# Feed-forwards whose input is turned unnormed, with the reciprocal roots multiplied in behind the first product

## The reference

```python
def rmsnorm(x, g):
    xf = x.astype(jnp.float32)
    y = xf * lax.rsqrt(jnp.mean(xf * xf, axis=-1, keepdims=True) + NORM_EPS)
    return (y * g.astype(jnp.float32)).astype(x.dtype)

def conv_ffn(x, w_in, conv_w, conv_b, w_out):
    T = x.shape[1]
    gate, up = jnp.split(x @ w_in, 2, axis=-1)
    gp = jnp.pad(gate, ((0, 0), (CONV_W - 1, 0), (0, 0)))
    gc = conv_b
    for j in range(CONV_W):
        gc = gc + gp[:, j:j + T, :] * conv_w[j]
    h = jax.nn.gelu(gc) * up
    return h @ w_out
...
        x = x + rmsnorm(m, norm_g[layer, 1])
        f = conv_ffn(rmsnorm(x, norm_g[layer, 2]), ffn_w_in[layer], ffn_conv_w[layer],
                     ffn_conv_b[layer], ffn_w_out[layer])
        x = x + rmsnorm(f, norm_g[layer, 3])
```

## Time and profile before

| | us |
|---|---|
| median of 3 runs | 1328.93 |
| lowest, highest | 1328.87, 1329.26 |
| the profiled execution | 1331.13 |
| its span in the profile | 1329.2 |
| PE busy in it | 1300.9 (98%) |
| DVE busy | 948.4 (71%) |
| ACT busy | 668.1 (50%) |
| from the start of the first product with the diagonal to the first `second`, `ffn0` | 224.19 to 240.46 |
| the same, `ffn1` | 523.57 to 539.83 |

### The profile page before, as it was taken

The page is one execution under the profiler, slowest core; times in us unless marked ns, Lnnn a source line. Parts: engine busy times, 40 slices in busy tenths (PEclk is TensorE's granted clock), DMA queues, the critical chain, the costliest instruction groups (busy, mean ns, idle before and its releaser), DMA issues.

```text
span 1329.2 us, 23254 instructions
## 1 busy us (share of the span) xinstructions
PE 1300.9 (98%) x9190; PEld 1127.4 (85%) x9190; DVE 948.4 (71%) x1646; ACT 668.1 (50%) x1026; POOL 103.2 (8%) x106
## 2 busy tenths in 40 slices
PE   7999999999999999999999998999999999999999
PEld 7889988888888888888888886888888888888887
DVE  6995476877778765877776697866666796666664
ACT  4554326444446586444446476543344568543331
POOL 0005250010000020000001020000001042000000
PEclk9999999999999999999999999999999999999999
DMA  9531107655533423655542631956350431674610
GB/s 301 175 127 65 52 19 253 209 187 189 191 125 135 136 91 127 205 187 189 191 156 82 217 134 44 361 214 236 144 179 11 167 127 64 242 265 154 226 64 32
DMA packets 113350, 208.48 MB, mean 157 GB/s; under 512 B 3952, under 2 KB 57584, under 8 KB 112752
## 3 DMA queue, kind: packets, MB, share of 16 engines
q1 hardware_dynamic: 113264, 207.28, 45.2%
HBM read 206.21 MB, written 1.05 MB: 156 GB/s over the span
## 4 chain that ended last, share of the span: by engine, by line
PE 87%; DVE 6%; ACT 5%; DMA 1%; issue 1%; POOL 0%; SPq 0%; DVEq 0%; ACTq 0%; POOLq 0%
PE ps L1071 21%; PE ps L1018 19%; PE ps L923 10%; PE ps L1023 10%; PE ps L1113 2%; PE ps L1234 2%; PE ps L1499 2%; PE ps L1128 2%; PE ps L1408 1%; DVE Al L2774 1%; PE ps L994 1%; ACT Ah L1947 1%; PE ps L1543 1%; PE ps L847 1%; PE ps L1557 1%
## 5 line engine op out<-in xcount | busy, mean ns | idle before, releaser
L1018 PE MATMUL ps<-hTx,Ah 128*128 128x512 f32 x1088 | 270.7, 391 | 0.0
L2781 DVE TENSOR_TENSOR Al<-ringA,Ah 128x2048 fp32r<-128x2048 f32 x74 | 169.3, 2287 | 97.2 <-ACT Ah L1957 97.2
L1018 PEld LDWEIGHTS ps<-hTx,Ah 128*128 128x128 f32 x1088 | 199.7, 188 | 38.5
L1023 PEld LDWEIGHTS ps<-hTx,Al 128*128 128x128 f32 x1152 | 156.7, 190 | 10.6
L1992 ACT COPY xn<-ps 128x512 f32<-128x512 f32 x72 | 42.3, 587 | 243.4 <-PE ps L1023 236.2
L1023 PE MATMUL ps<-hTx,Al 128*128 128x256 f32 x1152 | 160.7, 282 | 0.0
L1957 ACT CAST Ah<-ringA 128x2048 fp32r<-128x2048 f32 x76 | 145.8, 1918 | 13.1 <-PE ps L923 6.5
L1966 ACT CAST Bh<-ringB 128x1024 fp32r<-128x1024 f32 (+1 forms) x76 | 107.1, 1409 | 89.4 <-PE ps L1071 89.2
L923 PE MATMUL ps<-Ah,hTx 128*128 128x512 f32 (+1 forms) x576 | 136.5, 387 | 2.9 <-ACT Ah L1947 1.4
L2788 DVE TENSOR_TENSOR Bl<-ringB,Bh 128x1024 fp32r<-128x1024 f32 (+1 forms) x76 | 127.0, 1671 | 10.8 <-ACT Bh L1966 10.3
L1071 PE MATMUL ps<-Bh,hidh 128*128 128x512 f32 x416 | 129.9, 392 | 1.1 <-issue 1.1
(11 more groups left out here) (464 smaller groups left out, 2059.5 us busy)
## 6 DMA issues: line engine op xcount, KB each, us to landing
ringA<-in_ffn_w_in SPq DMA_DIRECT2D x44, 1024.0 KB, 6.8
ringA<-in_mlp_w SPq DMA_DIRECT2D x32, 1024.0 KB, 7.4
ringB<-in_mlp_w SPq DMA_DIRECT2D x32, 1024.0 KB, 6.9
ringB<-in_ffn_w_out SPq DMA_DIRECT2D x44, 512.0 KB, 4.0
ringA<-in_diff_w_in SPq DMA_DIRECT2D x12, 1024.0 KB, 6.4
ringA<-in_dsa_w_in SPq DMA_DIRECT2D x8, 1024.0 KB, 6.2
ringA<-in_w_r SPq DMA_DIRECT2D x4, 1024.0 KB, 6.3
ringA<-in_w_v SPq DMA_DIRECT2D x4, 1024.0 KB, 6.9
```

Source lines behind the costliest of these rows:

```text
L1018: mm(o.rearrange("p (i t) -> p i t", i=2), w_hi, hTx[:, :, k * T:(k + 1) * T], start=(k == 0), stop=False)
L1023: last = mm(o[:, T:2 * T], Al[:, half, k * T + j * P:k * T + j * P + P], hTh[:, k, :], start=False, stop=(k == KT - 1))
L2781: V.tensor_tensor(a_split(w, Al, half), a_half(w, (a_at[w] + par) % 2, half), a_split(w, Ah, half).bitcast(F32), ALU.subtract).then_inc(al ...
```

## The change

`nf0` and `nf1` (the turned inputs of `ffn0` and `ffn1`) enter the table `LATE`, so `x` is turned by plain transpositions that wait for its halves alone. ACT no longer squares halves of `x` in between: it squares each whole tile (`whole`), tile 0 ahead of its `turned_split` and tile 1 behind it. DVE takes both reciprocals after its own `turned_split` and writes two scaled identities into `rdiag` (`root_diagonals`). PE multiplies a matrix of ones (`unity`, set by POOL) with `rdiag` behind `first_of_all`, which gives a 128x256 array with every token's reciprocal root in each partition; ACT copies it from PSUM to `rbc` (`spread_root`). DVE multiplies gate and up by `rbc` in each half, ahead of `conv`. In the last half the gate is multiplied from PSUM and the gelu's result once more, in place of up. Seven `keep` products ahead of the turning become one. `rest_part(w, 0)` moves ahead of `res_norm`, and `first_of_all` waits for the rests in two steps.

The core of the diff:

```diff
-        LATE = {"n1": 1, "n2": 2, "n3": 3, "nm0": 0, "nm1": 0}
+        LATE = {"nf0": 0, "n1": 1, "nf1": 0, "n2": 2, "n3": 3, "nm0": 0, "nm1": 0}
...
+                            if t == 0 and k == KT - 1 and name in ("nf0", "nf1"):
+                                keep(1, 0)
...
                     pe.wait_ge(ah_rdy, S0[w] + 1)
-                    pe.wait_ge(al_rdy, S0[w] + 1)
                     for k in range(KT):
                         if k % 2 == 0:
                             pe.wait_ge(ha_rdy, 4 * TI[n_in] + k // 2 + 1)
+                        if nf == 1 and k == 0:
+                            pe.wait_ge(rb["al"], n + 1)
+                        elif k == (4 if nf == 1 else 0):
+                            pe.wait_ge(al_rdy, S0[w] + 1)
...
                     last.then_inc(f1_rdy, 1)
+                    if nf == 1:
+                        pe.wait_ge(rb["one"], n + 1)
+                        pe.wait_ge(rb["diag"], n + 1)
+                        mm(ps[:, 2, 0:T], unity, rdiag, start=True, stop=True).then_inc(rb["ps"], 1)
...
-            keep(7, 7)
+            keep(1, 7)
             turn16("nf0")
...
                 own(0)
-                summed(0, 0)
                 own(1)
-                summed(0, 1)
-                summed(1, 0)
-                summed(1, 1)
+                whole(mi, 0)
+
+            def whole(mi, t):
+
+                act.wait_ge(x_done, x_at(mi, t, 1))
+                square(xn[:, t, :], x[:, t, :], 8 + t)
+                A_(st[:, 2 + t:3 + t], hs[:, 8 + t:9 + t], ACT.Sqrt, bias=eps, scale=1.0 / D
+                   ).then_inc(rms_rdy, 1)
+
+            def spread_root(n):
+
+                act.wait_ge(rb["ps"], n + 1)
+                nc.scalar.copy(rbc, ps[:, 2, 0:T]).then_inc(rb["sb"], 1)
...
             res_norm(0)
             turned_split("nf0", "g0_ffn")
+            whole(MI["o0"], 1)
             ffn_start("ffn0", 1)
+            spread_root(0)
             ffn("ffn0", True)
...
+            pool.wait_ge(tp_rdy, 4 * (TI["o0"] + 1))
+            G.memset(unity, 1.0).then_inc(rb["one"], 1)
...
+                rest_part(w, 0).then_inc(rb["al"], 1)
                 dve.wait_ge(sq_rdy, 2 * mi + 1)
                 link(weighted(0, hi))
...
                 summed(1, lo)
-                norm(following, [0])
                 summed(1, hi)
                 dve.wait_ge(x_done, x_at(mi, 1))
-                rest_part(w, 0)
-                norm(following, [1])
                 rest_part(w, 1).then_inc(al_rdy, 1)
+
+            def root_diagonals(name):
+
+                dve.wait_ge(rms_rdy, 2 * NI[name] + 2)
+                link(V.reciprocal(st[:, 4:6], st[:, 2:4]))
+                for t in range(NT):
+                    last = V.tensor_scalar(rdiag[:, t * P:(t + 1) * P], ident, st[:, 4 + t:5 + t],
+                                           None, ALU.mult)
+                last.then_inc(rb["diag"], 1)
...
+                    gate = gup[:, 0, :]
                     if direct is None:
-                        gate = gup[:, 0, :]
                         sums(ch, half, gup)
+                        ins = V.tensor_tensor(gup, gup, rbc2, ALU.mult)
+                    elif ch:
+                        dve.wait_ge(gate_rdy, INST.index(w) + 1)
+                        ins = V.tensor_tensor(gate, direct[:, 0, :], rbc, ALU.mult)
                     else:
-                        gate = direct[:, 0, :]
...
+                        dve.wait_ge(f1_rdy, 2 * g0 + 1)
+                        dve.wait_ge(rb["sb"], INST.index(w) + 1)
+                        ins = V.tensor_tensor(gup, direct, rbc2, ALU.mult)
+                    ins.then_inc(hm_rdy, 1)
+                    dve.wait_ge(hm_rdy, ch * 2 + (2 * g0 + half + 1))
...
+                            up = gup[:, 1, :]
+                            if last and half:
+                                up = single_at(ch, half)[:, 1, :]
+                                link(V.tensor_tensor(ge[:, half, :], ge[:, half, :], rbc, ALU.mult))
                                 dve.wait_ge(f1_rdy, n)
```

More of the change, by code:

```diff
@@ L236, in program @@
         rs_rdy = sem("rs_rdy")
+        hm_rdy = sem("hm_rdy")
+        rb = {n: sem("rb_" + n) for n in ["one", "al", "diag", "ps", "sb"]}
         uq_in = sem("uq_in")
@@ L521, in program @@
         ht = xnflat[:, 0:512]
+        rbc, rdiag, unity = (rows[:, ROW["lnx_w"][0] + o:ROW["lnx_w"][0] + o + n]
+                             for o, n in ((0, T), (T, T), (2 * T, P)))
+        rbc2 = rbc.unsqueeze(1).to_broadcast([P, 2, T])
         gc = xnflat[:, 512:1024].rearrange("p (g n) -> p g n", g=2)
@@ L1901, in own @@
                     whole_root(10 + t, 4 * t + 2, 4 * t + 1).then_inc(msd_rdy, 1)
-                def summed(t, half):
-                    o = slice(512 * half, 512 * half + 512)
-                    act.wait_ge(x_done, x_at(mi, t, half))
-                    square(xn[:, t, o], x[:, t, o], 8 + 4 * t + 2 * half)
-                    if half:
-                        whole_root(2 + t, 10 + 4 * t, 9 + 4 * t).then_inc(rms_rdy, 1)
-                    else:
-                        part_mean(9 + 4 * t, 8 + 4 * t)
                 own(0)
-                summed(0, 0)
                 own(1)
-                summed(0, 1)
-                summed(1, 0)
-                summed(1, 1)
+                whole(mi, 0)
[7 more added lines that the diff above has]
+                nc.scalar.copy(rbc, ps[:, 2, 0:T]).then_inc(rb["sb"], 1)
             def job(j, *copies, b=None):
@@ L2351, in _ @@
             turned_split("nf1", "g1_ffn")
+            whole(MI["o1"], 1)
             ffn_start("ffn1", 1)
+            spread_root(1)
             ffn("ffn1", True, "din")
@@ L2582, in _ @@
                 rest_slot(a_at["wo1"], half)
+            pool.wait_ge(pre["ov"], 16)
+            G.memset(unity, 1.0).then_inc(rb["one"], 1)
             pool.wait_ge(x_done, x_at(MI["ffn1"], 1))
@@ L2668, in first_halves, with res_norm @@
                                     ).then_inc(wm_rdy, 1)
-            def res_norm(mi, gain, following, w):
+            def res_norm(mi, gain, w):
                 lo, hi = slice(0, 512), slice(512, D)
@@ L2823, in conv @@
                     direct = single_at(ch, half)
+                    gate = gup[:, 0, :]
                     if direct is None:
-                        gate = gup[:, 0, :]
                         sums(ch, half, gup)
-                    else:
-                        gate = direct[:, 0, :]
-                        if ch:
-                            dve.wait_ge(gate_rdy, INST.index(w) + 1)
-                        else:
-                            dve.wait_ge(f1_rdy, 2 * g0 + 1)
+                        ins = V.tensor_tensor(gup, gup, rbc2, ALU.mult)
+                    elif ch:
+                        dve.wait_ge(gate_rdy, INST.index(w) + 1)
+                        ins = V.tensor_tensor(gate, direct[:, 0, :], rbc, ALU.mult)
+                    else:
+                        dve.wait_ge(f1_rdy, 2 * g0 + 1)
[3 more added lines that the diff above has]
+                    dve.wait_ge(hm_rdy, ch * 2 + (2 * g0 + half + 1))
                     V.tensor_scalar(o, gate, colx(cw, f + 2 * F), colx(cb, f), ALU.mult, ALU.add
@@ L2867, in step @@
                             wid = T
-                            direct = single_at(ch, half)
-                            up = gup[:, 1, :] if direct is None else direct[:, 1, :]
-                            if direct is not None:
+                            up = gup[:, 1, :]
+                            if last and half:
+                                up = single_at(ch, half)[:, 1, :]
+                                link(V.tensor_tensor(ge[:, half, :], ge[:, half, :], rbc, ALU.mult))
                                 dve.wait_ge(f1_rdy, n)
@@ L3185, in _ @@
             rest_slot(a_at["wo0"] + 1, 1)
-            res_norm(0, "g0_res", "nf0", "ffn0")
+            res_norm(0, "g0_res", "ffn0")
             turned_split("nf0", "g0_ffn")
+            root_diagonals("nf0")
             ffn_start("ffn0", 1)
@@ L3375, in _ @@
             rest_slot(a_at["wo1"] + 1, 1)
-            res_norm(2, "g1_res", "nf1", "ffn1")
+            res_norm(2, "g1_res", "ffn1")
             turned_split("nf1", "g1_ffn")
+            root_diagonals("nf1")
             ffn_start("ffn1", 1)
```

## The result

| | us |
|---|---|
| the changed kernel, median of 10 runs | 1332.95 (1331.76 to 1334.51) |
| the kernel before, 10 runs beside them | 1329.91 (1328.87 to 1331.02) |
| ratio, with its 95% interval | 1.0027 (1.0019 to 1.0035) |
| the profiled execution, its span | 1331.77, 1329.9 |

Slower by 0.27%, and a second set of 11 runs gave 1332.42 against 1329.33, 1.0021 (1.0012 to 1.0030). The forecast was 1330.0 with a range of 1326.0 to 1332.8: the measured median lies just above the range, at rival (c).

The account below looks back on a forecast made before the run. PE's stream or its waits were taken as the bound, with DVE's string setting the first second product. -1.56 - 1.56 + 0.25 + 1.5 = -1.4 us gave 1327.6; one or two slow stretches gave 1329.2 or 1330.8, middle 1330.0, range 1326.0 to 1332.8.

Parts of the forecast that it names:

- rival (c): Each of the three long PE waits is followed by a slow-clock stretch of 1.6 us: 1332.4; chance 18%.
- The turning starts earlier: At the start of ffn0, turning ends at 224.15 and first_of_all starts 4.2 us earlier than 228.32.
- ACT keeps part of it: Ahead of the rounding, ACT's new square and root leave its string with DVE 2.3 us of the 3.9 gained.
- The new product and its copy: Behind first_of_all: ones product 0.46 us, ACT's copy about 0.45; second rounding releases DVE about 0.1 after the rest.
- DVE's string: To the first hidden values: 8.24 grows to 8.95 us; first second product 1.56 earlier per feed-forward, PE waiting 2.7.
- Inside the loop: Each half pays 0.88 us of DVE's 1.22 idle, leaving 0.34; cost zero.
- The last half: At the feed-forward ends, DVE's extra 1.5 us costs 1.5 in ffn1 (PE wait 2.0) and about 0.25 in ffn0.
- The sum: Over the whole kernel, gains and tail costs without the clock add to -1.4 us, giving 1327.6.
- The clock: Behind the long PE waits: 1.6 us per slow stretch, 65% for each 2.7 wait, half for 2.0; one or two likeliest.
- rival (a): PE is slowed early, by the turning at the start of ffn0, not late, and nothing is lost: 1327.6; chance 10%.

Follow-up runs that it names:

- e6: The changed kernel without ACT's square of x's tile 1, whose tokens take tile 0's roots: 1332.36 us, ratio 1.0022.
- e10: e6 with ACT's rounding of the first down weights put ahead of its copy of the spread roots: 1328.20 us, ratio 0.9988.
- e7: The changed kernel without DVE's multiplication by the roots in chunks 1 to 9 of each feed-forward: 1333.08 us, ratio 1.0024.
- e4: The kernel before with one filler product of seven left ahead of the transpositions in both layers: 1332.15 us, ratio 1.0018.
- e8: The kernel before with DVE's rest of the next layer's weight moved behind the last hidden values of ffn1: 1328.93 us, ratio 0.9994.
- e13: The kernel before with DVE's rest of gate weights behind the first hidden values, and its next-layer rest behind ffn1's last ones: 1327.55 us, ratio 0.9988.
- a0: The changed kernel timed again, unaltered, beside the kernel before: 1332.42 us, ratio 1.0021.
- e3: The changed kernel with DVE's rest of the next layer's weight moved behind the last hidden values of ffn1: 1329.36 us, ratio 0.9998.
- e1: The changed kernel with five unread products filling PE's wait ahead of the first second product: 1329.54 us, ratio 1.0000.
- e9: The changed kernel with DVE's rest of the next chunk's first gate weights behind chunk 0's first hidden values, both layers: 1327.96 us, ratio 0.9989.

## Why the prediction missed

**The turning starts earlier: right.** 4.2 us predicted, 3.9 measured.

**ACT keeps part of it: right.** The string over ACT and DVE was to keep 2.3 of 3.9; DVE's first rest starts at 227.88 for 232.12 - 1.83 = 230.29, 2.4 earlier.

**The new product and its copy: the size right, the weight of it missed.** I had the rounding behind the copy release DVE 0.1 us after the rest; the trace shows 0.24. That it lies so close was in the text, but not that it would bound the string alone if the square went: e6 and e10 showed that.

**DVE's string: right.** A gain of 1.56 predicted for each feed-forward, 1.48 measured; the wait 2.7 predicted, 2.54 measured. The multiplication takes 0.68 for 0.69. (The working has a slip that changes nothing: its terms add to 8.93 and not 8.95.)

**Inside the loop: right.** Cost zero. DVE's idle time fell from 1.22 to 0.50 where I left 0.34, and e7 shows that the multiplications could go without a gain.

**The last half: right for `ffn1`.** PE waits 2.02 there for a predicted 2.0 and starts 1.51 us later for 1.5. In `ffn0` it waits 0.24 for the predicted 0.25 and its products end 0.36 late, and the residual behind them is another 0.33 late, which I had not seen: one of DVE's additions takes 1.11 us at 411.44 where the others take 0.75. It runs under a cast of POOL (409.26 to 412.01), which starts with DVE's multiplications (409.22) where before it started 0.65 ahead of them. In all thirteen profiles where the two overlap, it takes 1.10 to 1.13; in the four where the cast has ended 0.1 us ahead of it (the kernel before, e4, e8, e13) it takes 0.75. The three multiplications just ahead of it, which read PSUM, run beside the same cast in both kernels and take 1.94 for three each time.

**The sum: nearly right.** With the clock left out the change brings 2 x 1.48 - 0.36 - 0.33 - 1.51 = 0.76 us, for 1.4 predicted.

**The clock: the step that failed.** I put 65% on each of the two waits of 2.7, since the trace of before had one case, took "one or two stretches" as the likeliest and put the term at their middle, 2.4 us. In the five profiles with a wait of 2.5 us ahead of the first `second` (after, a0, e3, e6, e7) each of the ten such waits is followed by a stretch, and no run of a0 or of the changed kernel has a mean clock that would allow fewer than two stretches. The price of one, 1.6, was right (1.64 and 1.59 in the trace after, 1.45 by e1). The tail's wait of 2.0 was followed in three of seven profiles (a0, e6, e10; not after, e1, e7, e9), near the half I gave it. So the term measured 2 x 1.6 + 0.8 = 4.0 in place of 2.4, the 0.8 being an estimate: half of 1.6. The forecast should have been 1327.6 + 0.6 + 4.0, about 1332.2. That is nearly rival (c), which I held at 18%; its 1332.4 was the nearest to the result, though it wanted the third stretch in every run, and it came so near partly by luck, since the base was low.

**The base was low, too.** All this stands on 1328.93, the median of three runs of before (1328.87 to 1329.26). Ten runs of it have a median of 1329.91, and the later groups 1329.2 to 1329.4. That is the part of the miss, up to 1.0 us, which has nothing to do with the change. The runs of before fall into two kinds: at a mean clock of 1.0 their medians are 1328.9 to 1329.2 in the four groups, at 0.998 and 0.999 1330.4 to 1331.3. The three runs have times of the first kind. The stretch at 20 to 24 goes with it: it stands in ten of the seventeen profiles. It isn't the whole difference. In the traces about 1.2 us come behind PE's wait near 20, and about 0.6 stand ahead of it already; that wait ends at 19.5 to 20.6 in the ten with a stretch and at 18.8 to 20.0 in the seven without. Why is open.

Which sign the change has depends on what it is joined with: 0.2% slower as it was made, level with the two waits filled (e1), and 0.1 to 0.2% faster than e13 when both have DVE's order turned.

## What to carry to other kernels

When a change shortens PE's string more than the string it meets, the difference comes back as a wait of PE, and on this kernel a wait of 2.5 us cost another 1.6 us behind it. So before making PE ready earlier, move what is not needed at that point (here 2.29 us of DVE's rest for the next chunk) out of the string it will wait for, and fill what wait remains with unread products. Look at the instruction queued behind each new wait, too: the copy that waited for the product with ones held back a rounding that needed nothing from it.

## What the runs showed of the hardware

- Every stretch of low clock in the seventeen profiles lasts 3.4 us at 1.2 GHz. Waits of PE of 2.54 us were followed by one ten times in ten; waits of 1.85 (start of the program) ten times in seventeen; of 2.0 (tail) three in seven; of 3.23 and 3.24 (e4) once in two; of 1.43 (at 464 in the trace after), 1.38, 1.03 and less, never. The length of the wait alone doesn't decide it; what does is open.
- Where the low clock begins differs too. Behind the waits of 2.54 us it began 0 to 1.0 us after PE had started again (238.0 for 237.15 in the trace after, 238.2 for 238.17 in e3), in the tail 1.2 to 1.5 us after, and in e4 at 521.85, 0.35 us before PE's wait ended at 522.20. It ended by itself; behind the 2.54 us waits PE was busy throughout.
- The sixteen transpositions with two fillers at the turning were followed by no low clock in any profile of the changed kernel (1.00 in the window at 220), so rival (a) falls. That transpositions don't count as busy for the clock, as the Trainium skill has it (TensorE: Matmul & The Clock Gate, "Part 4: PE-mode transpose"), was not seen at this size.
- A DVE addition of 128x512 with both arrays in SBUF took 1.10 to 1.13 us beside a POOL cast in thirteen of thirteen profiles, and 0.75 in the four where the cast had just ended; multiplications that read PSUM were not longer beside it. That the cast is the cause fits all seventeen, but no run moved the cast alone.
